# Trunk kernel: where twenty row sums, the column jobs and the first expert weights stand around the attention

## The chip, the cores and the metric

The kernel runs on one core of a Trainium2 chip, in one launch. The metric is the device time of that launch in microseconds (us); the times below are those of the core.

## What is computed

```python
for i in range(2):                       # DEPTH
    ml = silu(c) @ mod_w[i] + mod_b[i]   # (1024) @ (1024, 6144): shifts, scales and gates
    sh1, sc1, g1, sh2, sc2, g2 = split(ml, 6)
    hl = xl * (1 + sc1) + sh1
    yl = differential_attention(hl, context) if i == 0 else pooling(hl)
    xl = layer_norm(ALPHA * xl + (1 + g1) * yl)
    y2 = moe(xl * (1 + sc2) + sh2)       # 16 experts, top 2, three 1024 x 1024 matrices each
    xl = layer_norm(ALPHA * xl + (1 + g2) * y2)
```

There are 256 latent and 256 context tokens of width 1024, all in float32. The weights of 2 x 16 experts are most of what is read.

## The kernel before

All large weights come in **units** of 2 MB (128 x 4096 float32, 2.10 million bytes) into a buffer `ring` of 11 slots. An expert is 6 units, so layer 0 has the units 0 to 95 and unit v goes into slot `FREE[v % 11]`. SyncE (SP) issues all these loads in one fixed order, `LOADS` and then expert by expert, and waits ahead of each (`slot_free`, `early_used`) until its slot is free. One load that waits holds back all behind it.

The vector c @ mod_w is not multiplied on TensorE but summed on VectorE (DVE): a **sum** takes one unit of mod_w (two halves of 1 MB, slots 2 and 3 in turn) and adds its eight 128 x 512 blocks, each times a column of c (`unit_sum`, `half_sum`, L1340 and L1342). There are 20 of them, numbered 0 to 19. TensorE (PE) then folds four sums at a time over the partitions into bank 7 (`row_batch`, L638), `rows_sum` adds the bias (L1359), and small PE products and DVE copies bring the rows into the forms that are needed later: the **jobs** (`job`, `job_out`): columns (`cols_0`), a part of the router (`rpart_0`), the gates (`gt_0`, `g1_0`, `g1_1`). The early part of the kernel runs so:

- projections for k, q and v in groups of 7 us on PE, while DVE makes the first `EARLY_SUMS` sums and two rotary batches (`rope_batch`, L1380 to L1383);
- 16 attention **steps** s (`STEPS`): in each, PE makes a further projection group (steps 0 to 9 only), the scores of step s (L722), the transposes of s-2 (L582) and the values of s-3 (L740, bank 5). DVE takes maxima (L1469), forms the difference of the two softmaxes (L1480) and, in steps 0 to 9, one sum. ScalarE (ACT) takes exponentials (L1166), copies the transposes (L1160) and squares and copies the values (L1174, L1176);
- the heads are normed and turned, and multiplied with attn_wo in four products `project(t, h)` (L759); DVE makes sums 18 and 19 beside them;
- the first layer norm, the router (`route`), and then the experts (L902 gathers, L910 products).

The engines run their own lists in order, and semaphores join them. Loads can run ahead of the experts by the 11 slots at most, since unit v + 11 waits until unit v is used (`used`).

## Time and profile before

| | |
|---|---|
| device time, 3 runs | 1201.13 us (1200.76 to 1202.65) |
| the profiled execution's own time | 1202.47 us |
| its span in the trace | 1200.6 us |
| PE / DVE / ACT busy | 94% / 30% / 14% |
| read from HBM | 476.18 MB |
| granted PE clock, mean | 0.983 |

Busy shares are over the whole span. The times in the rows are counted from the span's start. The attention, the experts and the change of layer have different limits, so the mean shares say little.

### The profile page before, as it was taken

What the parts mean: (1) busy time and instruction counts of PE and PEld (TensorE: products, weight loads), DVE (VectorE), ACT (ScalarE), POOL (GpSimd) and SP (SyncE); (2) the same over time, 40 slices, a digit from 0 to 9 for tenths busy, and PEclk for the clock granted to TensorE, in tenths of its full rate; (3) what the DMA queues carried; (4) which work ended last, traced back from release to release, by engine and by line L of the source; (5) the groups of instructions that cost most, each with busy time, mean ns of one, the idle gap of its engine ahead of it and who ended that gap; (6) DMA issues with size and microseconds to landing.
All of it is one profiled execution on the core that took longest, in us unless ns stands there. A gap on an engine that the chain in (4) does not pass through costs nothing.

```text
span 1200.6 us, 12399 instructions
## 1 busy us (share of the span) xinstructions
PE 1133.3 (94%) x5282; PEld 493.3 (41%) x5282; DVE 362.8 (30%) x733; ACT 166.8 (14%) x397; POOL 8.0 (1%) x10
## 2 busy tenths in 40 slices
PE   8997998899999999999998889999999999988986
PEld 3543554545444333343333227543333433333322
DVE  1569899663111111111111115212111111111113
ACT  1201233514100000001000005200000100000000
POOL 0000000000000000000000010000000000000000
PEclk9998999899999999999999999999999999999999
DMA  9999897983999999999999999999999999999994
GB/s 387 407 376 379 289 361 269 400 321 158 431 429 430 433 429 430 430 431 430 431 430 430 431 424 430 424 429 432 431 429 432 430 430 433 430 430 430 431 430 182
DMA packets 41017, 480.17 MB, mean 400 GB/s; under 512 B 5120, under 2 KB 6400, under 8 KB 9472
## 3 DMA queue, kind: packets, MB, share of 16 engines
q1 hardware_dynamic: 39904, 476.91, 94.7%
q10 hardware_dynamic: 1056, 2.43, 0.7%
q8 instruction: 44, 0.72, 0.2%
q14 instruction: 13, 0.11, 0.0%
HBM read 476.18 MB, written 1.05 MB: 397 GB/s over the span
## 4 chain that ended last, share of the span: by engine, by line
PE 74%; DMA 18%; DVE 6%; ACT 1%; issue 1%; another core or an unknown queue 0%; SPq 0%; DVEq 0%
PE ps L910 44%; DMA ring<-in_moe_wu 16%; PE ps L902 5%; PE ps L918 4%; PE ps L664 3%; DMA ring<-in_mod_w 2%; PE ps L759 2%; PE ps L667 2%; DVE ring L1342 1%; PE ps L722 1%; PE ps L607 1%; PE ps L670 1%; PE ps L740 1%; DVE modp L1342 1%; PE ps L928 1%; PE ps L582 1%
## 5 line engine op out<-in xcount | busy, mean ns | idle before, releaser
L910 PE MATMUL ps<-ring,tra 128*64 128x512 f32 x2048 | 453.9, 597 | 24.2 <-DMA ring<-in_moe_wu 19.3
L910 PEld LDWEIGHTS ps<-ring,tra 128*64 128x64 f32 x2048 | 147.6, 138 | 322.3 <-issue 281.1
L910 PE MATMUL ps<-ring,work 128*64 128x512 f32 x1024 | 226.8, 595 | 1.9 <-DVE work L1693 1.9
L910 PEld LDWEIGHTS ps<-ring,work 128*64 128x64 f32 x1024 | 71.6, 137 | 135.6 <-issue 133.3
L1237 ACT ACTIVATE work<-ps 128x512 f32<-128x512 f32 x32 | 19.1, 597 | 506.5 <-PE ps L910 506.5
L1691 DVE TENSOR_TENSOR work<-work,ps 128x512 f32<-128x512 f32 x32 | 22.0, 687 | 205.7 <-PE ps L910 205.7
L1230 ACT ACTIVATE tra<-ps,cols 128x128 f32<-128x128 f32 x128 | 48.1, 456 | 255.3 <-PE ps L902 255.3
L1688 DVE TENSOR_TENSOR work<-ps,work 128x512 f32<-128x512 f32 x32 | 22.1, 691 | 202.1 <-ACT work L1237 202.1
L902 PEld LDWEIGHTS ps<-extra,xn 128*128 128x128 f32 x512 | 61.0, 195 | 24.3 <-issue 22.7
L902 PE MATMUL ps<-extra,xn 128*128 128x128 f32 x512 | 66.9, 285 | 1.4 <-DVE extra L1601 1.4
L918 PE MATMUL ps<-work,extra 64*128 64x512 f32 x256 | 63.6, 615 | 1.6 <-DVE work L1697 1.6
L664 PE MATMUL ps<-ring 128*128 128x512 f32 x128 | 58.6, 608 | 0.0
L1697 DVE TENSOR_TENSOR work<-ps,gt 128x512 f32<-128x512 f32 x16 | 11.1, 691 | 107.9 <-PE ps L910 107.9
L1697 DVE TENSOR_TENSOR work<-ps,rows 128x512 f32<-128x512 f32 x16 | 11.1, 691 | 107.9 <-PE ps L910 107.9
L1342 DVE SCALAR_TENSOR_TENSOR ring<-ring,cols 128x512 f32<-128x512 f32 x56 | 42.1, 752 | 2.1
L1693 DVE COPY work<-ps 128x512 f32<-128x512 f32 x32 | 22.1, 691 | 51.0 <-PE ps L928 51.0
L664 PEld LDWEIGHTS ps<-ring 128*128 128x128 f32 x128 | 24.0, 194 | 31.8 <-issue 31.8
L1342 DVE SCALAR_TENSOR_TENSOR extra<-ring,cols,extra 128x512 f32<-128x512 f32 x42 | 31.6, 752 | 3.9 <-DMA ring<-in_mod_w 2.5
L1342 DVE SCALAR_TENSOR_TENSOR modp<-ring,cols,modp 128x512 f32<-128x512 f32 x42 | 31.6, 752 | 1.5
L918 PEld LDWEIGHTS ps<-work,extra 64*128 64x128 f32 x256 | 22.0, 186 | 22.0 <-issue 15.1
L1676 DVE COPY extra<-ps 128x256 f32<-128x256 f32 x32 | 13.6, 424 | 48.4 <-PE ps L934 48.4
L667 PE MATMUL ps<-ring 128*128 128x512 f32 x64 | 28.1, 592 | 0.0
(192 smaller groups left out, 729.2 us busy)
## 6 DMA issues: line engine op xcount, KB each, us to landing
ring<-in_moe_wg SPq DMA_DIRECT2D x64, 2048.0 KB, 29.6
ring<-in_moe_wu SPq DMA_DIRECT2D x63, 2048.0 KB, 29.7
ring<-in_moe_wd SPq DMA_DIRECT2D x63, 2048.0 KB, 30.0
ring<-in_mod_w SPq DMA_DIRECT2D x40, 1024.0 KB, 9.6
ring<-in_mod_w SPq DMA_DIRECT2D x4, 2048.0 KB, 17.1
ring<-in_attn_wqkv SPq DMA_DIRECT2D x4, 2048.0 KB, 11.4
ring<-in_attn_wo SPq DMA_DIRECT2D x2, 2048.0 KB, 11.2
ring<-in_tokens SPq DMA_DIRECT2D x4, 512.0 KB, 18.0
```

What stands on the lines that cost most here:

```text
L664: return mm(bank(acc_bank(g)), w[:, k, t * P:t * P + P], hT[:, k, :], start=first, stop=end)
L667: return mm(bank(acc_bank(g)), hT[:, k, t * P:t * P + P], rhs, start=first, stop=end)
L759: last = mm(bank(2 * t + h), oT[t][:, k, :], wo[:, k, :], start=(k == 0), stop=(k == KT - 1))
L902: last = mm(bank(bk, 0, P, k * P, k * P + slots), xn[:, c0:c0 + P], sgat[:, t, 0:slots], start=(t == 0), stop=(t == TT - 1), skip_group_ch ...
L910: last = mm(ps[SLOTS * h:SLOTS * h + SLOTS, b, :], lhs(k0 + k), w[:, k, h * NB:(h + 1) * NB], start=(k0 + k == 0), stop=(k0 + k == KT - 1) ...
L918: last = mm(bank(2 * t + h), sw[SLOTS * h:SLOTS * h + SLOTS, t * P:t * P + P], ysb[SLOTS * h:SLOTS * h + SLOTS, :], start=False, stop=True ...
L1230: nc.scalar.activation(xg[i // 2 % 2][:, kk, :], bank(bk, k * P, k * P + P), ACT.Identity, bias=one(bcol[2 * layer], kk, 1), scale=one(aco ...
L1342: ins = v_.scalar_tensor_tensor(out=acc, in0=w[:, k, :], scalar=ck, in1=acc, op0=ALU.mult, op1=ALU.add)
L1688: v_.tensor_tensor(hmid, bank(4), sig, ALU.mult).then_inc(sem("silu_ready"), 1)
L1691: v_.tensor_tensor(hmid, hmid, bank(5), ALU.mult).then_inc(sem("h_ready"), 1)
L1693: v_.tensor_copy(work[:, NB:2 * NB], bank(7)).then_inc(sem("hTt_copied"), 1)
L1697: v_.tensor_tensor(ysb, bank(6), gt[layer], ALU.mult).then_inc(sem("ys_ready"), 1)
```

## The change

The tables that set the order get other numbers. Seven sums stand ahead of the steps and nine in the steps 0 to 8; both rotary batches come ahead of sum 5. Of the other four, sums 16 and 17 follow the norm of the heads, sum 18 is split between the attention's norm and the router, and sum 19 is made in the first expert, in slot 3 itself, and folded by a job of its own (`row_1`). The column jobs leave the steps and go between the projections; fold 4 goes behind the router's logits. Values alternate between banks 5 and 6, ACT copies before it squares, and DVE makes the last copy of transposes. Units 1 to 9 are now issued among the last sums. Unit 10, whose slot sum 19 holds, is issued behind unit 15.

```diff
-FREE = (10, 4, 8, 5, 9, 6, 7, 2, 3, 1, 0)
+FREE = (10, 4, 8, 5, 9, 6, 7, 1, 0, 2, 3)
...
-BATCH_AT = {6: 0, 10: 1, 15: 2, 19: 3}
-
-EARLY_SUMS = 8
-STEP_SUMS = 10
-
-LOADS = [("q", 0), 0, 1, ("v", 0), 2, "rows", 3, 4, ("k", 1), 5, 6, 7, 8, ("q", 1), 9, "ahead", 10, 11, 12, ("v", 1), 13, 14,
-         ("wo", 0), 15, 16, 17, ("wo", 1), "x", 18, 19]
-AHEAD = 1
-
-
-JOBS = ("cols_0", "rpart_0", "gt_0", "g1_0", "g1_1", "cols_2", "cols_1", "joint_0", "joint_1", "rpart_1", "gt_1",
+BATCH_AT = {8: 0, 12: 1, 16: 2, 20: 3}
+
+EARLY_SUMS = 7
+STEP_SUMS = 9
+ROPES_AT = 5
+
+LOADS = [("q", 0), 0, 1, ("v", 0), 2, "rows", 3, 4, ("k", 1), 5, 6, ("q", 1), 7, "ahead", 8, 9, 10, 11, ("v", 1), 12, 13,
+         ("wo", 0), 14, 15, "x", 16, 17, ("wo", 1), ("e", 1), ("e", 2), ("e", 3), ("e", 4), ("e", 5), ("e", 6), 18, 19,
+         ("e", 7), ("e", 8), ("e", 9)]
+AHEAD, ISSUED = 1, 10
+LATE_UNIT = 10
+AFTER_UNIT = 15
+
+
+JOBS = ("g1_0", "g1_1", "cols_0", "rpart_0", "gt_0", "row_1", "cols_2", "cols_1", "joint_0", "joint_1", "rpart_1", "gt_1",
         "lng_0", "lng_1", "lnb_0", "lnb_1")
-JOB_AT = {10: (0,), 11: (1,), 12: (2,)}
-JOB_BANK = (6, 6, 6, 2, 2, 7, 7, 7, 7, 7, 7, 7, 7, 7, 7)
-HEAD_BANK = ((6, 3), (4, 5))
+JOB_BANK = (2, 2, 6, 6, 5, 7, 7, 7, 7, 7, 7, 7, 7, 7, 7, 7)
+HEAD_BANK = ((1, 3), (4, 5))
 EARLY_JOBS = 5
-LATE_JOB = {(0, e): EARLY_JOBS + e - 1 for e in range(1, 7)} | {(1, e): EARLY_JOBS + 5 + e for e in range(1, 5)}
+LATE_JOB = {(0, e): EARLY_JOBS + e for e in range(7)} | {(1, e): EARLY_JOBS + 6 + e for e in range(1, 5)}
...
+        last_sum = ring[:, 3 * UNIT:3 * UNIT + NB]
...
                 elif v in (7, 8):
-                    sp.wait_ge(sem("half_summed"), 2 * (NSUM - 8 + v))
-                elif v < RING:
-                    sp.wait_ge(sem("unit_used"), NA - RING + v + 1)
+                    early_used(sp, ("wo", v - 7))
+                elif v == 9:
+                    sp.wait_ge(sem("half_summed"), 2 * (NSUM - 1))
+                elif v == LATE_UNIT:
+                    sp.wait_ge(sem("job_done"), EARLY_JOBS + 1)
...
-                for n in range(AHEAD if layer == e == 0 else 0, EU):
-                    load_unit(layer, e, n)
+                for n in range(EU):
+                    v = first_unit(layer, e) + n
+                    if v >= ISSUED and v != LATE_UNIT:
+                        load_unit(layer, e, n)
+                    if v == AFTER_UNIT:
+                        load_unit(0, LATE_UNIT // EU, LATE_UNIT % EU)
...
+                elif isinstance(what, tuple) and what[0] == "e":
+                    load_unit(0, what[1] // EU, what[1] % EU)
...
-                pe.wait_ge(sem("half_summed"), 2 * (BATCH * b + BATCH))
+                units = min(BATCH, NSUM - 1 - BATCH * b)
+                pe.wait_ge(sem("half_summed"), 2 * (BATCH * b + units))
                 if b == SUMS0 // BATCH:
                     pe.wait_ge(sem("rows_ready"), 1)
-                for g in range(4):
+                for g in range(units):
...
-                pe.wait_ge(sem("aT_copied"), s + 1)
+                if s < NS - 1:
+                    pe.wait_ge(sem("aT_copied"), s + 1)
+                else:
+                    pe.wait_ge(sem("last_aT_copied"), 1)
                 out_of_psum(9 if j == 0 else 19)
-                if s:
-                    pe.wait_ge(sem("o_copied"), s)
+                if s >= 2:
+                    pe.wait_ge(sem("o_squared"), s - 1)
                 for k in range(KEYT):
-                    last = mm(bank(5, 0, P, 0, P), aT[s % 2][:, k * P:k * P + P], vv[:, k, hh * P:hh * P + P],
+                    last = mm(bank(5 + s % 2, 0, P, 0, P), aT[s % 2][:, k * P:k * P + P], vv[:, k, hh * P:hh * P + P],
...
-                    pe.wait_ge(sem("job_out"), EARLY_JOBS)
-                pe.wait_ge(sem("oT_copied"), 2 * (t + 1))
+                    pe.wait_ge(sem("job_out"), 2)
                 for k in range(KT):
+                    if k % 4 == 0:
+                        pe.wait_ge(sem("oT_copied"), 2 * t + k // 4 + 1)
...
+                elif kind == "row":
+                    pe.wait_ge(sem("half_summed"), 2 * NSUM)
+                    r0 = C_ROW + 31 - SUMS[NSUM - 1][1] // 4
+                    last = mm(bank(bk, 96, 128), cst[:, r0:r0 + 32], last_sum, start=True, stop=True, skip_group_check=True)
...
                     values(NS - 3)
+                    pe.wait_ge(sem("exp_done"), 2 * NS)
+                    job(0)
                     turn_probs(NS - 1)
                     values(NS - 2)
                     turn_heads(0)
                     values(NS - 1)
-                    job(3)
                     project(0, 0)
                 elif s < NS:
                     if s >= 2:
                         turn_probs(s - 2)
                     if s >= 3:
                         values(s - 3)
-                for i in JOB_AT.get(s, ()):
-                    job(i)
-            pe.wait_ge(sem("aT_copied"), NS)
-            pe.wait_ge(sem("o_copied"), NS)
+            job(1)
+            pe.wait_ge(sem("o_squared"), NS)
+            job(2)
             turn_heads(1)
             project(0, 1)
-            job(4)
-            row_batch(4)
-            NT_BANK = (4, 6, 5, 7)
+            job(3)
+            NT_BANK = ((4, 6, 5, 0), (4, 6, 5, 7))
...
             project(1, 0)
-            turn_normed(0, 0)
+            job(4)
             project(1, 1)
-            pe.wait_ge(sem("rows_ready"), 2)
...
+                if layer == 0:
+                    pe.wait_ge(sem("job_out"), EARLY_JOBS)
+                turn_normed(layer, 0)
+                keep_clock(5 if layer else 1, 3)
                 turn_normed(layer, 1)
-                keep_clock(0, 1)
+                keep_clock(1, 1)
...
+                if layer == 0:
+                    row_batch(4)
...
+            def copy_probs(s):
+                act.wait_ge(sem("aT_done"), s + 1)
+                nc.scalar.copy(aT[s % 2], bank(4)).then_inc(sem("aT_copied"), 1)
+
+            def copy_values(s):
+                j, t, h = STEPS[s]
+                hh = HPJ * j + h
+                o = bank(5 + s % 2, 0, P)
+                act.wait_ge(sem("pv_done"), s + 1)
+                nc.scalar.copy(osb[:, t, hh * P:hh * P + P], o).then_inc(sem("o_copied"), 1)
+                act.wait_ge(sem("o_copied"), s + 1)
+                nc.scalar.activation(o, o, ACT.Square, accum_out=ss[:, t, hh:hh + 1]).then_inc(sem("o_squared"), 1)
+
+            for s in range(NS):
                 for kind, i in FILL[s]:
                     if kind == "g":
                         evacuate(i)
-                if 2 <= s < NS + 2:
-                    act.wait_ge(sem("aT_done"), s - 1)
-                    nc.scalar.copy(aT[s % 2], bank(4)).then_inc(sem("aT_copied"), 1)
-                if s < NS:
-                    act.wait_ge(sem("nb_ready"), s + 1)
-                    for n in range(2):
-                        j, t, h = STEPS[s]
-                        total = lead[:, t, HPJ * j + h:HPJ * j + h + 1] if n == 0 else sm[:, s % 2, 1:2]
-                        nc.scalar.activation(pr[s % 2][:, n, :], bank(score_bank(s) + n), ACT.Exp,
-                                             bias=nb[:, s % 2, n:n + 1], scale=SCALE, accum_out=total).then_inc(sem("exp_done"), 1)
-                if s == NS - 1:
-                    heads_std(0)
-                if s >= 3:
-                    j, t, h = STEPS[s - 3]
-                    hh = HPJ * j + h
-                    act.wait_ge(sem("pv_done"), s - 2)
-                    nc.scalar.activation(bank(5, P, 2 * P), bank(5, 0, P), ACT.Square,
-                                         accum_out=ss[:, t, hh:hh + 1]).then_inc(sem("o_squared"), 1)
-                    nc.scalar.copy(osb[:, t, hh * P:hh * P + P], bank(5, 0, P)).then_inc(sem("o_copied"), 1)
-                if s == NS + 1:
-                    copy_heads(0)
+                if s >= 2:
+                    copy_probs(s - 2)
+                act.wait_ge(sem("nb_ready"), s + 1)
+                for n in range(2):
+                    j, t, h = STEPS[s]
+                    total = lead[:, t, HPJ * j + h:HPJ * j + h + 1] if n == 0 else sm[:, s % 2, 1:2]
+                    nc.scalar.activation(pr[s % 2][:, n, :], bank(score_bank(s) + n), ACT.Exp,
+                                         bias=nb[:, s % 2, n:n + 1], scale=SCALE, accum_out=total).then_inc(sem("exp_done"), 1)
+                if 3 <= s < NS - 1:
+                    copy_values(s - 3)
+            heads_std(0)
+            copy_probs(NS - 2)
+            copy_values(NS - 4)
+            copy_values(NS - 3)
+            copy_heads(0)
+            copy_values(NS - 2)
+            copy_values(NS - 1)
...
-                if n == 6:
-                    rope_batch(0)
+                if n == ROPES_AT:
+                    for batch in range(2):
+                        rope_batch(batch)
                 unit_sum(n)
-            rope_batch(1)
...
-                for i in JOB_AT.get(s, ()):
-                    job_out(i)
                 if s == NS - 1:
                     heads_variance(0)
                 if s == NS:
                     norm_heads(0)
-            job_out(3)
+            dve.wait_ge(sem("aT_done"), NS)
+            v_.tensor_copy(aT[(NS - 1) % 2], bank(4)).then_inc(sem("last_aT_copied"), 1)
+            dve.wait_ge(sem("pv_done"), NS - 1)
+            job_out(0)
             heads_variance(1)
             norm_heads(1)
-            for n in range(EARLY_SUMS + STEP_SUMS, NSUM):
-                unit_sum(n)
-            job_out(4)
+            unit_sum(NSUM - 4)
+            job_out(1)
+            job_out(2)
+            unit_sum(NSUM - 3)
+            job_out(3)
...
+                        if (t, h) == (1, 0):
+                            half_sum(2 * (NSUM - 2))
                     spread(0, t)
                     deviation(0, t)
                     if t == 0:
-                        rows_sum(1)
+                        job_out(4)
...
+                if layer == 0:
+                    half_sum(2 * (NSUM - 2) + 1)
...
+                dve.wait_ge(sem("row_done"), -(-NSUM // BATCH))
                 pick_rows(0, 0)
                 pick_rows(1, 1).then_inc(sem("sgat_ready"), 1)
                 pick_weights(0).then_inc(sem("ssc_ready"), 1)
+                if layer == 0:
+                    rows_sum(1)
...
+                if layer == 0:
+                    rows_scaled()
...
+                if q == 0:
+                    half_sum(2 * (NSUM - 1))
...
+                if q == 0:
+                    half_sum(2 * (NSUM - 1) + 1)```

The DVE's list ahead of the steps (a sum is a row `TENSOR_SCALAR` and a row `SCALAR_TENSOR_TENSOR` x7, a rotary batch three rows `TENSOR_TENSOR`). Before, from sum 5:

```order
L1340 TENSOR_SCALAR ring<-ring,cols 128x512
L1342 SCALAR_TENSOR_TENSOR ring<-ring,cols 128x512 x7
L1380 TENSOR_TENSOR ring<-ring 128x4x256
L1382 TENSOR_TENSOR ring<-ring 128x1024
L1383 TENSOR_TENSOR ring<-ring 128x4x256
L1340 TENSOR_SCALAR ring<-ring,cols 128x512
L1342 SCALAR_TENSOR_TENSOR ring<-ring,cols 128x512 x7
L1340 TENSOR_SCALAR ring<-ring,cols 128x512
L1342 SCALAR_TENSOR_TENSOR ring<-ring,cols 128x512 x7
L1380 TENSOR_TENSOR ring<-ring 128x1024
```

These are sum 5, batch 0, sums 6 and 7, and the start of batch 1. And now, from sum 4, which both have:

```order
L1371 TENSOR_SCALAR ring<-ring,cols 128x512
L1373 SCALAR_TENSOR_TENSOR ring<-ring,cols 128x512 x7
L1412 TENSOR_TENSOR ring<-ring 128x4x256
L1414 TENSOR_TENSOR ring<-ring 128x1024
L1415 TENSOR_TENSOR ring<-ring 128x4x256
L1412 TENSOR_TENSOR ring<-ring 128x1024
L1414 TENSOR_TENSOR ring<-ring 128x1024
L1415 TENSOR_TENSOR ring<-ring 128x1024
L1371 TENSOR_SCALAR ring<-ring,cols 128x512
```

Both batches, which the scores of step 0 wait for, stand ahead of sum 5, and there is one sum less.

SP's loads from attn_wo's first half on (`in_mod_w` halves are sums, `in_moe_*` are expert units). Before:

```order
L429 DMA ring<-in_attn_wo 128x4096
L429 DMA ring<-in_mod_w 128x2048 x6
L429 DMA ring<-in_attn_wo 128x4096
L429 DMA xn<-in_x 128x2x1024
L429 DMA ring<-in_mod_w 128x2048 x4
L429 DMA ring<-in_moe_wg 128x4096
L429 DMA ring<-in_moe_wu 128x4096 x2
L429 DMA ring<-in_moe_wd 128x4096 x2
```

And now:

```order
L433 DMA ring<-in_attn_wo 128x4096
L433 DMA ring<-in_moe_wg 128x4096
L433 DMA ring<-in_moe_wu 128x4096 x2
L433 DMA ring<-in_moe_wd 128x4096 x2
L433 DMA ring<-in_moe_wg 128x4096
L433 DMA ring<-in_mod_w 128x2048 x4
L433 DMA ring<-in_moe_wg 128x4096
L433 DMA ring<-in_moe_wu 128x4096 x2
L433 DMA ring<-in_moe_wd 128x4096
L433 DMA ring<-in_moe_wg 128x4096 x2
L433 DMA ring<-in_moe_wu 128x4096 x2
L433 DMA ring<-in_moe_wd 128x4096 x3
```

Units 1 to 6 went ahead of the sums 18 and 19, and the last row holds the units 10, 16 and 17.

PE's list from the turned heads on (L759 and L774 are the projections, 8 matmuls each; L638 and L651 folds). Before:

```order
L582 MATMUL ps<-cst,ring 128x128 x8
L759 MATMUL ps<-ring,work 128x512 x8
L781 MATMUL ps<-rows,cst 128x512
L638 MATMUL ps<-modp,cst 32x512 x2
L638 MATMUL ps<-extra,cst 32x512 x2
L759 MATMUL ps<-ring,tra 128x512 x8
L582 MATMUL ps<-cst,xn 128x128 x8
L759 MATMUL ps<-ring,tra 128x512 x8
L607 MATMUL ps<-cst 128x512 x3
```

And now:

```order
L774 MATMUL ps<-ring,work 128x512 x8
L796 MATMUL ps<-rows,cst 128x512
L781 MATMUL ps<-cst,rows 128x28 x4
L594 MATMUL ps<-cst,ring 128x128 x8
L774 MATMUL ps<-ring,work 128x512 x8
L824 MATMUL ps<-cols,rwa 32x1 x8
L774 MATMUL ps<-ring,tra 128x512 x8
L815 MATMUL ps<-rows,cst 64x512 x2
L774 MATMUL ps<-ring,tra 128x512 x8
L594 MATMUL ps<-cst,xn 128x128 x8
L619 MATMUL ps<-cst 128x512 x3
```

The fold and the turn of the normed rows (L582 from xn) left the space between the projections, and three column jobs (L781, L824, L815) came in.

## Rows read from the trace of the kernel before

**Rows 1.** Windows: busy of PE, PEld, DVE, ACT, POOL; PE clock, DMA share, GB/s.

```profile
274.00:292.00 18.00, 16.67 (x119) 11.77 (x120) 8.01 (x41) 9.54 (x22) 0.00 (x0) 0.93 0.01 2
292.00:593.00 301.00, 300.06 (x1499) 121.41 (x1495) 50.44 (x118) 25.22 (x60) 0.00 (x0) 1.00 1.01 429
...
716.00:760.00 44.00, 40.59 (x250) 32.28 (x252) 21.62 (x71) 20.98 (x39) 2.00 (x2) 0.96 1.01 430
```

**Rows 2.** Timeline of SP: start, time over the merged issues.

```profile
267.13 24.35 SPq L429 DMA_DIRECT2D ring<-in_moe_wd  x2
```

**Rows 3.** Chain that ended last: start, time, what.

```profile
597.03 44.54 DMA ring<-in_moe_wu
...
1120.81 49.09 DMA ring<-in_moe_wu
```

**Rows 4.** Timeline of DVE ahead of the steps; [idle before].

```profile
77.10 5.56 DVE L1342 SCALAR_TENSOR_TENSOR ring<-ring,cols 128x512 f32<-128x512 f32 x7
86.73 0.49 DVE L1340 TENSOR_SCALAR ring<-ring,cols 128x512 f32<-128x512 f32 x1 [4.07 <-DMA ring<-in_mod_w]
...
92.65 1.22 DVE L1380 TENSOR_TENSOR ring<-ring 128x1024 f32<-128x1024 f32 x1
...
96.18 0.48 DVE L1340 TENSOR_SCALAR ring<-ring,cols 128x512 f32<-128x512 f32 x1
```

**Rows 5.** Timeline of PE up to step 1.

```profile
75.06 0.62 PE L638 MATMUL ps<-modp,cst 128*32 128x512 f32 x2 [1.72 <-DVE extra L1342]
...
108.14 1.07 PE L638 MATMUL ps<-ring,cst 128*32 128x512 f32 x8 [4.34 <-DVE ring L1342]
111.67 2.08 PE L722 MATMUL ps<-ring 64*128 64x512 f32 x4 [2.46 <-DVE ring L1383]
113.67 8.29 PE L664 MATMUL ps<-ring 128*128 128x512 f32 x16
121.89 1.13 PE L722 MATMUL ps<-ring 64*128 64x512 f32 x4
```

**Rows 6.** Timeline of DVE: the maxima of steps 1, 9, 10, 13, 15.

```profile
123.06 1.22 DVE L1469 TENSOR_REDUCE small<-ps 128x2 f32<-128x1024 f32 x1 [1.86 <-PE ps L722]
...
198.23 1.22 DVE L1469 TENSOR_REDUCE small<-ps 128x2 f32<-128x1024 f32 x1 [0.17 <-PE ps L722]
...
206.58 1.22 DVE L1469 TENSOR_REDUCE small<-ps 128x2 f32<-128x1024 f32 x1
...
218.33 1.22 DVE L1469 TENSOR_REDUCE small<-ps 128x2 f32<-128x1024 f32 x1 [0.37 <-PE ps L722]
...
224.05 1.22 DVE L1469 TENSOR_REDUCE small<-ps 128x2 f32<-128x1024 f32 x1 [0.65 <-PE ps L722]
```

**Rows 7.** Window of the steps 10 to 15, columns as in rows 1.

```profile
200.00:224.00 24.00, 20.62 (x113) 12.46 (x110) 20.39 (x43) 13.56 (x47) 0.00 (x0) 0.79 1.01 426
```

**Rows 8.** Timeline of ACT behind the last step.

```profile
226.98 1.28 ACT L1144 ACT_TABLE_LOAD   x1
...
228.81 0.59 ACT L1160 COPY tra<-ps 128x512 f32<-128x512 f32 x1
```

**Rows 9.** Timeline of PE from the last steps to the fourth projection.

```profile
202.68 1.94 PE L766 MATMUL ps<-cst,rows 128*128 128x28 f32 x8
...
235.60 7.03 PE L759 MATMUL ps<-ring,work 128*128 128x512 f32 x16
...
250.21 1.02 PE L781 MATMUL ps<-rows,cst 128*128 128x512 f32 x2
...
260.07 7.03 PE L759 MATMUL ps<-ring,tra 128*128 128x512 f32 x16
```

**Rows 10.** Timeline of DVE at the router.

```profile
277.35 0.19 DVE L1619 TENSOR_TENSOR small<-ps,rb 128x32 f32<-128x32 f32 x1 [3.78 <-PE ps L876]
```

**Rows 11.** Timeline of PE from the ranks to the first expert.

```profile
281.48 0.84 PE L886 MATMUL ps<-small,cst 128*128 128x16 f32 x6
...
287.47 13.95 PE L910 MATMUL ps<-ring,tra 128*64 128x512 f32 x64
```

More of the change, by code:

```diff
@@ L1152, in copy_heads @@
                                          ACT.Copy, scale=subln).then_inc(sem("oT_copied"), 1)
-            for s in range(NS + 3):
+            def copy_probs(s):
[10 more added lines that the diff above has]
+            for s in range(NS):
                 for kind, i in FILL[s]:
@@ L1417, in job_out @@
                     v_.tensor_copy(gt[int(w)], src).then_inc(sem("job_out"), 1)
+                elif kind == "row":
+                    part = rows[1][96:128, :]
+                    dve.wait_ge(sem("rows_ready"), 2)
+                    v_.tensor_tensor(part, part, ps[96:128, JOB_BANK[i], :], ALU.add).then_inc(sem("job_out"), 1)
                 elif kind == "lnb":
@@ L1525, in normed_out @@
                 dve.wait_ge(sem("nT_done"), 4 * layer + 2 * t + 2)
-                v_.tensor_copy(nT[:, 4:8, t * P:t * P + P], bank((6, 7)[t]).rearrange("p (k t) -> p k t", k=4))\
+                v_.tensor_copy(nT[:, 4:8, t * P:t * P + P], bank((6, 0 if layer == 0 else 7)[t]).rearrange("p (k t) -> p k t", k=4))\
                     .then_inc(sem("nT_dve"), 1)
@@ L1671, in route @@
                 weights_out(NE * layer)
+                if layer == 0:
+                    rows_scaled()
             def weights_out(q):
```

26 lines of the change are left out of this document (11 added, 15 removed).

## Prediction, on record before the run

> **What bounds the kernel now.** I read the windows first. From 292 us on the DMA engines run at share 1.01 and 429 GB/s, also while the layers change, whatever PE does [rows 1]. The chain that ended last confirms it: from 597 us it waits for expert weights, and again from 1121 us to the last units [rows 3]. PE starts with a full ring, uses experts faster than they come, has eaten up its stock by 597 us, and from there each unit's arrival sets the pace. So the end is fixed by one thing: the time at which the stream of loads last stood still, and how much was loaded by then. All loads behind that point follow without a gap.
>
> The stream last stands still from 274 to 292 us: share 0.01 [rows 1]. SP's row says why. It issues unit 10 at 267.1 and its next, unit 11, 24.3 us later [rows 2], because unit 11 needs the slot of unit 0. All 11 slots are full, and the first expert must use one. Its first products start at 287.47 [rows 11]. So idle DMA in the attention costs nothing by itself. **What counts is T, the start of the first expert, and the number of units ahead of it.** If T moves by x and n units fewer are loaded by then, the end moves by x plus n times 2.10 MB / 429 GB/s = 4.9 us.
>
> **What the change does to T**, from front to back. The shift is against the times before; minus is earlier.
>
> *A, start of the steps.* Before, PE ended its group of step 0 at 108.14 - 4.34 = 103.8, then waited 4.34 us for sum 7 (the fold of sums 4 to 7) and 2.46 us for batch 1; it had also waited 1.72 us for the fold of sums 0 to 3 [rows 5]. Now the first fold stands two groups later, the second in step 2, and both batches ahead of sum 5: sum 4 ends at 77.10 + 5.56 = 82.7, two batches of 3.5 us (92.65 to 96.18) end at 89.7 [rows 4], long before the scores. These start at 103.8 - 1.7 = 102.1 in place of 111.67. DVE is ready as well: two sums of 5.9 us (86.73 to 92.65) behind 89.7 end at 101.6 [rows 4]. The 4.07 us wait for sum 5's load is filled by the batches. Then the clock. The scores after the wait took 2.08 us against 1.13 in step 1, and the next group 8.29 against 7.03 for 16 matmuls of the same shape [rows 5, 9]. Without the wait step 1's scores end at 102.1 + 1.1 + 7.0 + 1.1 = 111.3 in place of 123.0. Shift -11.7.
>
> The Trainium skill (TensorE: Matmul & The Clock Gate, the section What's actually happening) says the same of the cause: an idle array falls to half clock, 1.2 of 2.4 GHz, and work brings it back. By it there is no ramp left at 103 us. The trace agrees so far as the rows behind the wait are the slow ones.
>
> *B, steps 1 to 10.* From step 1's maxima to step 9's there are 75.2 us [rows 6]; content is the same (8 sums, 2 batches, 2 folds), so -11.7 holds at step 9. Step 9 loses its sum: before, step 10's maxima came 8.35 us later. DVE would need 8.35 - 5.9 = 2.45, but PE must make scores, a transpose, values and now fold 3: three times about 1.0 and 0.5. I take 3.5, so -4.9. Shift -16.6.
>
> *C, steps 10 to 15.* 17.5 us for five steps, with three column jobs and a PE clock of 0.79 [rows 6, 7]. The two steps without a job, 218.33 to 224.05, took 2.86 us each. Five of them are 14.3; ACT's exponentials and copies now have one semaphore more in each step, so I take 15.0. Bounds: 14.3, and 17.5 if nothing is won. -2.5. Shift -19.1.
>
> *D, last maxima to first projection.* 11.55 us before (224.05 to 235.60) [rows 6, 9]. Job `g1_0` (1.0 us) moves in front of the last transpose, into the time in which PE waits for the table load of 1.28 us at 226.98 and the copy at 228.81 [rows 8]; the last copy goes to DVE; the values of two steps no longer share a bank; and the projection starts on half of the turned heads. Following ACT from the exponentials: table 1.3, root 0.2, copy 0.6, then transpose 0.9, values 1.0, heads 0.9, values 1.0 on PE: 8.8. -2.8, bounds 0 and -3.5. Shift -21.9: the first projection starts at 213.7.
>
> The copy at 228.81 starts 0.55 us after the table load is over [rows 8]. The Trainium skill (ScalarE: Activation LUTs, What ACT_TABLE_LOAD costs) adds a drain of about 1.4 us to each switch of tables; by that D would be -1.4 and the time 1.4 us longer. No such gap stands in the rows, so I leave it out.
>
> *E, the four projections.* From 235.60 to 260.07 + 7.03 = 267.1 [rows 9]. Out: the fold between them (1.0) and the turn of the normed rows (1.0, now in the wait behind the fourth projection). `g1_1` (1.02) stays. In: `cols_0` (1.0; at most the 1.94 of its row), `rpart_0` 0.4 and `gt_0` 1.0. +0.5, at most +1.4. Is DVE late anywhere? By my estimate from the same row lengths the heads are normed about 4 us behind the start of the first projection, sum 16 and `cols_0` end at 225.5, sum 17 at 231.5, and the t = 0 half of the norm at 236.5, all before PE needs them. Then `gt_0` out at 239, 2.2 us of gating, and the half sum of sum 18, 3.0: to 244.3. The fourth projection ends at 245.7. The cover is about 1.4 us thin; beyond it each us delays T. Shift -21.4.
>
> *F, norm, router, first expert.* The second half of sum 18 (3.0) lies in DVE's 3.78 us wait for the logits [rows 10]. Fold 4 (three matmuls, 0.75) stands ahead of PE's 16 residual products, whose end met the ranks at 281.48 [rows 11] without a gap: +0.8. `rows_sum` (0.75) lies beside the gather. Shift -20.6: **T = 266.9**.
>
> *G, units ahead.* Unit 10 is no longer loaded ahead of T: slot 3 holds sum 19. The 11 slots hold 10 units, so the stream has 2.10 MB less behind it when it goes on: **+4.9 us**. Is the stream still full by then? The last three slots come free at the end of the third and fourth projection (238.2, 245.7) and with sum 18 (277.35 - 0.7 - 21 = 256), and 4.9 us each end at 261, nine before T + 3.5 = 270.4. So DMA will idle again.
>
> Behind T: unit 15 is issued when unit 4 is used (T + 21), unit 10 when `row_1` is done (T + 25.5), and DMA has units 11 to 15 until T + 29. Unit 10 lands by T + 36, and the second expert needs it at T + 43. Sum 19's two halves lie in DVE's waits for products there.
>
> **Sum.** -11.7 - 4.9 - 2.5 - 2.8 + 0.5 + 0.8 + 4.9 = -15.7 us. Against the profiled execution's own 1202.47 (span 1200.6 and 1.9 around it) this gives 1186.8; it stood 1.3 above the median of the runs, so for the median 1201.13 - 15.7 = 1185.4. What no row covers (semaphores between the thinner waits) makes things rather later: I say 1186.
>
> **Rivals.**
> - *The attention gives less back.* In steps 1 to 9 PE and DVE both are full, and C, D and the thin cover in E rest on waits that get shorter. With C and D at zero and 1.5 us of DVE in E: -15.7 + 2.5 + 2.8 + 1.5 = -8.9, time 1192. For it: no row shows steps without these waits. Against: the two undisturbed steps at 2.86. 0.15.
> - *The slot costs nothing.* If the stream were not full at T before the change, or is not after it, G is no loss; time 1180.5. Against: 18 us of idle at share 0.01. 0.05.
> - *More is won.* C at 14.3, D at -3.5, E at 0, no delay in F: 1182 to 1183.5. 0.10.
> - *Slower.* Sum 18 is now issued behind units 3 to 6, on an SP queue that goes in order, and unit 6 waits for the turned heads (223.5). DVE has its first half inside the layer norm, in front of everything to T. It should land at 232 and is wanted at 241. Each us beyond 241 + 1.4 delays T; it decides from 15.7 us beyond, a landing at 258. For it: four waits ahead in one queue. Against: nothing in the queue is asked for later than 224. Similarly unit 10 behind `row_1` would have to stop the stream for 16 us. 0.03; near no change 0.02.
>
> **How the numbers follow.** The forecast as summed has 0.65. The range for 8 in 10 takes in the gain of the third rival and the loss of the first: 1181.5 to 1193. A measurement of this kernel can tell about 0.2% (2.4 us) from no change. Faster by more than that: 0.65 + 0.15 + 0.05 + 0.10 = 0.95; within it 0.02; slower 0.03.
>
> **What would show it.** A: no wait over 1 us before the first scores, which start near 102, and full clock there. B and C: last maxima near 205. D and E: first projection near 214, fourth over near 246. F: first expert products near 267. G: DMA share about 0 from 262 to 271, then 1.01 with no gap at T + 25, and SP waiting for the first expert with 10 units issued. The first expert 20.6 us earlier and the end only 15.7 earlier is the mark of the lost slot. Wrong would be: a DMA gap in the first two experts, DVE waiting for a `mod_w` load in the norm, or the end moving with something other than T.

## The result and the profile after

The changed kernel takes 1183.8 us (median of 4 runs, 1183.2 to 1185.0), the kernel before 1201.4 in the same session. The ratio is 0.9853, interval [0.9836, 0.9870]: 1.5% faster. The forecast said 1186.0 with a range of 1181.5 to 1193.0. The profiled execution has a span of 1181.8 us and its own time is 1183.56; before these were 1200.6 and 1202.47. So they fell by 18.8 and 18.9, where the prediction's sum said 15.7.

The windows, at the places that answer to [rows 1, 7], columns as there:

```profile
182.00:206.00 24.00, 22.72 (x136) 13.68 (x135) 22.19 (x46) 17.94 (x55) 0.00 (x0) 1.00 0.92 371
...
255.00:262.00 7.00, 6.28 (x57) 6.18 (x56) 5.17 (x28) 2.55 (x5) 0.00 (x0) 1.00 0.63 264
262.00:268.00 6.00, 6.00 (x37) 3.02 (x37) 2.17 (x8) 2.68 (x8) 0.00 (x0) 1.00 0.00 0
268.00:274.00 6.00, 6.00 (x32) 2.00 (x30) 2.57 (x4) 0.60 (x1) 0.00 (x0) 1.00 0.98 369
274.00:574.00 300.00, 297.51 (x1484) 119.19 (x1482) 54.78 (x125) 24.65 (x59) 0.00 (x0) 1.00 1.01 430
700.00:742.00 42.00, 38.95 (x247) 31.53 (x247) 22.49 (x73) 22.09 (x42) 0.00 (x0) 0.96 1.01 429
```

The window of the steps 10 to 15 now has a granted PE clock of 1.00 in place of 0.79 [rows 7]. The stream of loads last stands still from 262 to 268 (share 0.00) and then runs at 1.01 and 430 GB/s, also while the layers change. SP shows the same pause: unit 9 is the second issue of the first row, unit 11 comes when the first expert gives back a slot, and unit 10 is one of the three of the last row.

```profile
243.54 9.76 SPq L433 DMA_DIRECT2D ring<-in_moe_wu  x2
267.26 0.33 SPq L433 DMA_DIRECT2D ring<-in_moe_wd  x1
...
289.24 3.92 SPq L433 DMA_DIRECT2D ring<-in_moe_wd  x3
```

DVE's maxima of the steps 1, 9, 10 and 15, which answer to [rows 6]:

```profile
110.73 1.22 DVE L1505 TENSOR_REDUCE small<-ps 128x2 f32<-128x1024 f32 x1 [0.62 <-PE ps L735]
...
186.64 1.22 DVE L1505 TENSOR_REDUCE small<-ps 128x2 f32<-128x1024 f32 x1
189.43 1.23 DVE L1505 TENSOR_REDUCE small<-ps 128x2 f32<-128x1024 f32 x1 [0.27 <-PE ps L735]
...
202.46 1.23 DVE L1505 TENSOR_REDUCE small<-ps 128x2 f32<-128x1024 f32 x1
```

PE, which answers to [rows 5, 9, 11]: the scores of step 0, the first projection, `cols_0`, the fourth projection, fold 4 and the first expert.

```profile
101.43 1.13 PE L735 MATMUL ps<-ring 64*128 64x512 f32 x4
...
210.81 7.03 PE L774 MATMUL ps<-ring,work 128*128 128x512 f32 x16
218.54 1.82 PE L781 MATMUL ps<-cst,rows 128*128 128x28 f32 x8
...
236.38 7.13 PE L774 MATMUL ps<-ring,tra 128*128 128x512 f32 x16
...
253.01 0.62 PE L651 MATMUL ps<-modp,cst 128*32 128x512 f32 x2 [0.70 <-DVE extra L1373]
...
263.56 13.95 PE L930 MATMUL ps<-ring,tra 128*64 128x512 f32 x64
```

T, the start of the first expert, is 263.56 in place of 287.47: 23.9 us earlier. The end is 18.8 us earlier. The difference of 5.1 is the lost slot. In the chain that ended last, the waits for weights have moved forward; the last answers to that at 1120.81 in [rows 3]:

```profile
576.23 46.27 DMA ring<-in_moe_wu
...
1101.66 49.43 DMA ring<-in_moe_wu
```

### The profile page after: what moved, and what is told of

The parts are those of the page before. It is cut to its first block, busy times and chain, and to the rows that moved or that the text cites. A ratio compares the mean times of both kernels' runs of the same rounds, so it can differ in the third digit from the quotient of the medians.

```text
span 1181.8 us, 12403 instructions
## 1 busy us (share of the span) xinstructions
PE 1124.6 (95%) x5282; PEld 487.8 (41%) x5282; DVE 364.2 (31%) x735; ACT 167.0 (14%) x396; POOL 8.0 (1%) x10
## 4 chain that ended last, share of the span: by engine, by line
PE 75%; DMA 20%; DVE 3%; ACT 0%; issue 0%; another core or an unknown queue 0%; SPq 0%; DVEq 0%
PE ps L930 42%; DMA ring<-in_moe_wu 20%; PE ps L677 5%; PE ps L680 5%; PE ps L922 5%; PE ps L938 4%; PE ps L774 2%; PE ps L683 2%; PE ps L735 1%; PE ps L948 1%; PE ps L594 1%; PE ps L756 1%; PE ps L872 1%; PE ps L954 1%; DMA ring<-in_mod_w 1%; PE ps L627 1%
## 5 line engine op out<-in xcount | busy, mean ns | idle before, releaser
L930 PE MATMUL ps<-ring,tra 128*64 128x512 f32 x2048 | 454.5, 598 | 27.6 <-DMA ring<-in_moe_wu 22.0
L930 PEld LDWEIGHTS ps<-ring,tra 128*64 128x64 f32 x2048 | 146.5, 138 | 327.7 <-issue 281.9
L930 PE MATMUL ps<-ring,work 128*64 128x512 f32 x1024 | 226.8, 595 | 1.9 <-DVE work L1743 1.9
L930 PEld LDWEIGHTS ps<-ring,work 128*64 128x64 f32 x1024 | 71.6, 137 | 135.6 <-issue 133.3
L1373 DVE SCALAR_TENSOR_TENSOR ring<-ring,cols 128x512 f32<-128x512 f32 x63 | 47.4, 752 | 2.2
L1373 DVE SCALAR_TENSOR_TENSOR modp<-ring,cols,modp 128x512 f32<-128x512 f32 x42 | 31.6, 752 | 1.5
L683 PE MATMUL ps<-ring 128*128 128x256 f32 x128 | 28.1, 379 | 0.0
```

Source lines behind the costliest of these rows:

```text
L683: last = mm(bank(acc_bank(g), 0, P, n * TOK, (n + 1) * TOK), w[:, k, hd * P:hd * P + P], hT[:, k, 0:TOK], start=first and n == 0, stop=end ...
L930: last = mm(ps[SLOTS * h:SLOTS * h + SLOTS, b, :], lhs(k0 + k), w[:, k, h * NB:(h + 1) * NB], start=(k0 + k == 0), stop=(k0 + k == KT - 1) ...
L1373: ins = v_.scalar_tensor_tensor(out=acc, in0=w[:, k, :], scalar=ck, in1=acc, op0=ALU.mult, op1=ALU.add)
```

## The experiments

Each edits the changed kernel and computes the same. Ratios are against the kernel before, run in the same session (sessions 1 to 3: 1203.88, 1202.49 and 1202.28 us). "Base" is the changed kernel: span 1181.8, T 263.56. In the diffs "..." stands for lines left out.

Spans and T are read from one traced execution of each kernel. The medians, less base's 1183.8, give e1 +4.7, e2 +5.6, e3 +7.0, e4 +8.5, e5 +8.3, e6 +2.6, e7 +3.8, e8 +8.4 and e10 +14.5. The traced executions of e6, e7 and e8 are the lowest of theirs, so their span shifts are at the low end. The kernel before varied by 2.5 us between sessions (1201.4 to 1203.9), so ratios of different sessions can't be compared more finely than 0.2%.

### Is the end T plus 4.9 us for each unit not loaded ahead?

**One unit fewer ahead**, e1_nine_ahead: unit 9 waits for the slot of unit 0.

```diff
-         ("e", 7), ("e", 8), ("e", 9)]
-AHEAD, ISSUED = 1, 10
+         ("e", 7), ("e", 8),]
+AHEAD, ISSUED = 1, 9
...
                 elif v == 9:
                     sp.wait_ge(sem("half_summed"), 2 * (NSUM - 1))
+                    used(sp, 0)
```

> Unit 9 is no longer issued among the last sums but waits, like unit 11, until the first expert has used unit 0. Nothing in front of the experts changes. By my account (end = T less 4.9 us for each unit loaded ahead) the first expert's products stay at 263.6 us, the stream of loads has 2.10 MB more behind its last standstill, and the time is 1183.8 + 4.9 = 1188.7 us. The rival, that PE's own stock of loaded units matters little because the end is set by when PE starts, gives 1183.8.

1188.5 us, ratio 0.9877 [0.9862, 0.9892]. T is 263.63, as in base, and the span 1186.8: +5.0 for one unit. SP now waits from 243.6 to 267.7:

```profile
243.61 24.10 SPq L433 DMA_DIRECT2D ring<-in_moe_wu  x2
```

Term G holds, to 0.1 us.

**A later first expert**, e2_late_expert: five filler products in front of it, nothing else.

```diff
+                if layer == 0:
+                    pe.wait_ge(sem("routed"), 1)
+                    keep_clock(5, 5)
                 for e in range(NE):
                     expert(layer, e)
```

> Five more matmuls of 128x512 (0.91 us each as the fillers at 244.22 show) stand in front of the first expert of layer 0; their result is not used. T moves by 4.5 us, 10 units stay ahead. My account gives 1183.8 + 4.5 = 1188.3 us. Rival: PE waits for weights some 40 us in all later on, so it has room and 4.5 us of extra PE work ahead of the experts are swallowed: 1183.8.

1189.4 us, 0.9878 [0.9863, 0.9893]; T 269.48 (+5.9) and span 1187.7 (+5.9). The end moves with T, one for one. Here are PE's router products (3.84 us in base), the fillers and the first expert:

```profile
253.99 5.46 PE L872 MATMUL ps<-cst,work 128*128 128x128 f32 x32
265.09 4.46 PE L619 MATMUL ps<-cst 128*128 128x512 f32 x10
269.48 5.80 PE L930 MATMUL ps<-ring,tra 128*64 128x512 f32 x26
```

4.5 of the 5.9 us are the fillers. The rest was lost ahead of them, where the same 32 products took 1.6 us longer: the granted clock is 0.73 from 255 to 260, and 1.00 there in base.

**The ring not full at T**, e3_units_behind: the units 1 to 6 are issued behind the sums 18 and 19, as the kernel before had its sums first.

```diff
-         ("wo", 0), 14, 15, "x", 16, 17, ("wo", 1), ("e", 1), ("e", 2), ("e", 3), ("e", 4), ("e", 5), ("e", 6), 18, 19,
+         ("wo", 0), 14, 15, "x", 16, 17, ("wo", 1), 18, 19, ("e", 1), ("e", 2), ("e", 3), ("e", 4), ("e", 5), ("e", 6),
```

> Units 1 to 6 are issued behind sums 18 and 19, as before the change; all else stays. T stays at 263.6 us. By my account the ring must also be full at T + 3.5: sum 19's second half can be issued at 228.1, then nine units of 4.9 us end at about 274.5, where the stream of the changed kernel restarts at about 269: 5.5 us later, 1189.3 us, and no standstill ahead of the experts. If T alone decides: 1183.8. If the late sums delay DVE in the norm it would be the other way, T a little earlier, as sum 18 lands earlier.

1190.8 us, 0.9908 [0.9885, 0.9931]; T 263.58, unchanged, but span 1188.9 (+7.1; I had expected +5.5). The four half loads of the sums hold up the queue for 11.4 us while free slots stand empty behind them, and after that the windows have no pause (from 228 to 268 the DMA share is 1.01, and the last three are shown). Of its four runs one took 1196.1 us, the others 1190.5 to 1190.8. Why it is 1.6 us more than I had expected stays open.

```profile
217.09 11.38 SPq L433 DMA_DIRECT2D ring<-in_mod_w  x4
```

```profile
255.00:260.00 5.00, 4.28 (x39) 4.18 (x38) 3.68 (x22) 2.23 (x4) 0.00 (x0) 1.00 1.03 436
260.00:265.00 5.00, 5.00 (x41) 4.02 (x41) 3.66 (x16) 2.82 (x8) 0.00 (x0) 1.00 0.99 426
265.00:270.00 5.00, 5.00 (x26) 1.63 (x24) 0.00 (x0) 0.19 (x1) 0.00 (x0) 1.00 0.99 423
```

So the rule has a condition, that the ring is full before T, and this change meets it by its order of issue.

### What the parts of the change are worth

**One bank for the values**, e4_one_bank: the jobs stay where the change put them.

```diff
-                if s >= 2:
-                    pe.wait_ge(sem("o_squared"), s - 1)
+                if s:
+                    pe.wait_ge(sem("o_squared"), s)
...
-                    last = mm(bank(5 + s % 2, 0, P, 0, P), aT[s % 2][:, k * P:k * P + P], vv[:, k, hh * P:hh * P + P],
+                    last = mm(bank(5, 0, P, 0, P), aT[s % 2][:, k * P:k * P + P], vv[:, k, hh * P:hh * P + P],
...
-                o = bank(5 + s % 2, 0, P)
+                o = bank(5, 0, P)
```

> Values use bank 5 only again, and TensorE waits until ScalarE has squared the step before; all else as changed. If the alternating banks are what made the steps 10 to 15 take 13.0 us instead of my 15.0, they go back to 14.5 to 15 and the two values in front of the first projection wait for ScalarE as well (+1.5): the first expert at 263.6 + 3.3, time about 1187. If the banks matter only at the end: +1.5, 1185.3. If the pace came from the jobs and the clock: no change in the steps.

A miss in the time: 1192.3 us, 0.9913 [0.9896, 0.9929]; span 1190.6, +8.8. Steps 10 to 15 take 14.74 us against 13.03 (+1.7), as expected, at a granted clock of 1.00. From the last maxima (204.11) to the first projection (218.12) it is 14.0 against 8.35 (+5.7, where I had said +1.5). Another 1.6 us are lost at the router, as in e2 (5.47 us in place of 3.84). PE's timeline says why the last stretch grows: behind the last step it waits twice for ACT's square of the values before it may write the next ones into the only bank.

```profile
209.73 1.33 PE L756 MATMUL ps<-ring,tra 128*128 128x128 f32 x8 [2.37 <-ACT ps L1187]
210.85 1.92 PE L796 MATMUL ps<-rows,cst 128*128 128x512 f32 x2
...
217.16 1.13 PE L756 MATMUL ps<-ring,tra 128*128 128x128 f32 x8 [1.57 <-ACT ps L1187]
218.12 4.46 PE L774 MATMUL ps<-ring,work 128*128 128x512 f32 x10
```

In base the same values show no wait at all, and the job at L796 takes 1.02. The waits make idle PE, and the job behind the first runs at 1.92. I had costed the wait alone. Of the 5.7 the two waits are 3.9; the rest I can't split further. The kernel before, with one bank too, took 11.55 us for this stretch [rows 6, 9], less than the 14.0 here. So 5.7 is what the second bank is worth in the changed order, not its share of what the change gained.

**One bank, and the jobs back in steps 10 to 12**, e5_jobs_in_steps, on top of the last edit:

```diff
+JOB_AT = {10: (0,), 11: (1,), 12: (2,)}
-JOBS = ("g1_0", "g1_1", "cols_0", "rpart_0", "gt_0", "row_1", "cols_2", "cols_1", "joint_0", "joint_1", "rpart_1", "gt_1",
+JOBS = ("cols_0", "rpart_0", "gt_0", "g1_0", "g1_1", "row_1", "cols_2", "cols_1", "joint_0", "joint_1", "rpart_1", "gt_1",
...
-JOB_BANK = (2, 2, 6, 6, 5, 7, 7, 7, 7, 7, 7, 7, 7, 7, 7, 7)
+JOB_BANK = (6, 6, 6, 2, 2, 7, 7, 7, 7, 7, 7, 7, 7, 7, 7, 7)
...
```

> As the one-bank kernel, and the three column jobs are back in steps 10, 11, 12 (out of the space between the projections). The step without a sum stays. Before the change the three steps with jobs took 11.75 us against 2.6 each now: +3.9 us in the steps, and 1.7 + 0.3 + 1.0 = 3.0 us come back between the projections, so +0.9 against the one-bank kernel if those 11.75 us were the jobs' own. If most of them were the half clock that followed TensorE's wait for sum 17 in step 9, which is gone here, the steps grow by 1.5 us at most and the kernel is 1.5 us faster than the one-bank one.

1192.1 us, 0.9915 [0.9899, 0.9932]; span 1189.8, 0.8 less than with one bank alone. The steps get 3.1 us longer (189.21 to 207.06) and the way to the first projection 1.3 (to 222.34). The projections, without the jobs, get 3.3 shorter, and PE's 32 router products at L872 take 3.84 us, where with one bank alone they took 5.47. Without that last difference, which the edit doesn't touch, this kernel would be 0.9 us slower than the one-bank one, what the first theory said. The second theory is out: the steps grow by 3.1 us and not by 1.5 at most, at a granted clock of 1.00. So moving the jobs is worth 0.9 us at most by itself (the medians differ by 0.2). It frees the second bank, and the two together are worth 8 us. With the jobs in the steps, but no sum in step 9, the clock stays at 1.00, so the jobs alone don't bring the 0.79 of [rows 7].

```profile
190.00:207.00 17.00, 15.97 (x105) 10.30 (x106) 13.28 (x34) 12.12 (x39) 0.00 (x0) 1.00 0.91 389
205.00:222.00 17.00, 11.91 (x63) 9.29 (x63) 7.82 (x18) 9.07 (x27) 0.00 (x0) 0.80 0.63 255
```

**A sum back into step 9**, e8_sum_in_step9:

```diff
-STEP_SUMS = 9
+STEP_SUMS = 10
...
-            unit_sum(NSUM - 4)
```

> The changed kernel with a tenth sum put back into step 9 of the attention, as the kernel before had it, and taken out of those behind the steps. Theory: from step 9 to step 10 the maxima now go 2.8 us apart, and with a sum of four 1.46 us operations in front of them they go 8.3 to 9 us apart; TensorE waits inside that step, and its clock may fall in the steps behind it for another 1 to 2 us; the sums behind the steps stand beside other work, so nothing comes back there: the first expert starts 6 to 7 us later and the time is about 1190.5 us. Rival: the sum only changes its place, and what VectorE loses in step 9 it has less to do behind the steps: 1183.8 us.

1192.2 us, 0.9919 [0.9904, 0.9934]; span 1189.2 (+7.4), T 270.92 (+7.4, a little over the 6 to 7 that I had expected). The maxima of step 9, the sum (its seven operations) and the maxima of step 10, and the windows around them:

```profile
186.62 1.22 DVE L1505 TENSOR_REDUCE small<-ps 128x2 f32<-128x1024 f32 x1
189.58 5.48 DVE L1373 SCALAR_TENSOR_TENSOR modp<-ring,cols,modp 128x512 f32<-128x512 f32 x7
194.97 1.22 DVE L1505 TENSOR_REDUCE small<-ps 128x2 f32<-128x1024 f32 x1
```

```profile
190.00:198.00 8.00, 2.34 (x14) 1.39 (x13) 7.68 (x13) 2.13 (x7) 0.00 (x0) 0.79 1.03 441
198.00:206.00 8.00, 7.90 (x44) 5.61 (x42) 5.63 (x13) 5.89 (x20) 0.00 (x0) 0.78 0.93 393
```

The step takes 8.35 us again instead of 2.8 (+5.6). PE stands idle for 5.7 us of the first window, whose mean clock is 0.79, and though it is busy for 7.9 of the next 8 us, it is so at a mean of 0.78: the half clock, 1.2 of 2.4 GHz, up to 201 and the full one from 202 on. Steps 10 to 15 take 14.88 (+1.8). The rival, that the sum only changes its place, is out.

Is this wait also the source of the 0.79 of [rows 7]? That isn't shown. In the kernel before, PE has jobs to do beside sum 17. From 200.82 to 206.47 no row of it waits more than 0.24 us, and the clock is at half from 205 on, before its wait of 2.70 us begins at 206.47. Here are the windows of the kernel before, columns as in [rows 1]:

```profile
200.00:205.00 5.00, 4.66 (x26) 3.59 (x24) 4.82 (x7) 2.09 (x8) 0.00 (x0) 0.98 0.97 407
205.00:210.00 5.00, 2.30 (x8) 0.71 (x4) 4.72 (x14) 1.88 (x7) 0.00 (x0) 0.50 1.01 427
210.00:215.00 5.00, 5.00 (x33) 3.22 (x32) 3.39 (x9) 2.46 (x8) 0.00 (x0) 0.50 1.04 439
215.00:220.00 5.00, 5.00 (x33) 3.18 (x33) 4.21 (x10) 3.26 (x10) 0.00 (x0) 1.00 1.02 431
220.00:225.00 5.00, 4.66 (x30) 2.75 (x27) 4.20 (x8) 4.45 (x16) 0.00 (x0) 1.00 0.96 410
```

The jobs without the sum leave the clock at 1.00 (e5), and the sum without the jobs halves it behind a wait of 5.66 us (e8). Why it fell in the kernel before, with both, stays open. Nor can its price there be read from the total: steps 10 to 15 took 17.5 us with it, and 17.85 in e5 without it.

**Eight sums ahead**, e7_eight_ahead (`EARLY_SUMS = 8`, `STEP_SUMS = 8`):

> Eight sums ahead of the steps and eight in steps 0 to 7, the folds where the changed kernel has them. VectorE reaches step 0 5.9 us later; the scores stand ready at 101.4. If VectorE's total work sets T, the 5.9 us are won back in step 8, which has no sum; TensorE, which has a group of 7 us ahead of each scores, hides most of the lateness: T +2, time 1185.8. If a sum ahead of the steps costs its full length (as term A counted it): T +5.9, 1189.7.

1187.6 us, 0.9895 [0.9865, 0.9925]; span 1184.8 (+3.0), T 266.68. The maxima of step 1 come 6.8 us later (117.55) and those of step 10 only 3.1 later (192.54): the step that loses its sum gives part of it back. In step 1 DVE also waits 1.80 us for the next sum's load (at 111.64), since the loads keep their order. A sum ahead of the steps costs half of its 5.9 us in this trace. The six runs reach from 1186.7 to 1198.1, and their median lies midway between the two theories.

**The second rotary batch behind sum 6**, e6_ropes_last:

```diff
-                    for batch in range(2):
-                        rope_batch(batch)
+                    rope_batch(0)
                 unit_sum(n)
+            rope_batch(1)
```

> Batch 1 of the rotary work goes behind sum 6 again (batch 0 stays ahead of sum 5). VectorE has the same work and ends it at 102.3 us. TensorE is ready for the first scores at 101.4 and now has to wait for batch 1 until about 102.5: T +1.1 to +1.3 us, time 1185.0. If the place of the batches was what made the start of the steps early (the 10 us of term A), it would be +3.5 or more: 1187.5.

1186.4 us, 0.9875 [0.9859, 0.9892]; span 1183.1 (+1.3). The scores of step 0 wait 1.44 us for the batch, and T moves by 1.35, as expected. The median is less clear: the four runs reach from 1185.0 to 1189.2, the traced one took 1185.0, and the median of 1186.4 lies between the theory and its rival.

**A late load of sum 18**, e10_sums_behind_unit8. This makes the condition of the prediction's slower rival true.

```diff
-         ("wo", 0), 14, 15, "x", 16, 17, ("wo", 1), ("e", 1), ("e", 2), ("e", 3), ("e", 4), ("e", 5), ("e", 6), 18, 19,
-         ("e", 7), ("e", 8), ("e", 9)]
+         ("wo", 0), 14, 15, "x", 16, 17, ("wo", 1), ("e", 1), ("e", 2), ("e", 3), ("e", 4), ("e", 5), ("e", 6), ("e", 7), ("e", 8),
+         18, 19, ("e", 9)]
```

> The changed kernel with the loads of the sums 18 and 19 issued behind the units 7 and 8 and no longer ahead of them. It tests the slower rival of the prediction, a late load of sum 18 whose wait lies inside the norm. Theory: sum 18 is issued at about 244 us instead of 222, lands at 251 to 254, and VectorE, which takes its instructions in order, has the rows and the norm queued behind it: the first expert starts about 10 us later (1194.3 us), still less than before, since the ring is full by then. Rival: the sum's wait is covered by TensorE's projections: 1183.8 us.

1198.3 us, 0.9963 [0.9950, 0.9977]; span 1196.1 (+14.3), T 277.82 (+14.3; I had expected +10). DVE waits inside the norm, with everything to T queued behind:

```profile
254.13 0.49 DVE L1371 TENSOR_SCALAR extra<-ring,cols 128x512 f32<-128x512 f32 x1 [14.98 <-DMA ring<-in_mod_w]
```

In base this row starts at 239.27, 14.9 us earlier, and DVE then still waits 1.50 us for the fourth projection. That is the prediction's cover of 1.4. Beyond it each us counts: 13.4 us in the norm. The last 0.9 are at PE: after its wait of 14.6 us the turn of the normed rows took 1.97 us against 1.09 in base, the fillers behind it 1.56 against 1.02, and about 0.5 us came back in a shorter wait for DVE (0.24 against 0.70). The landing came at the late end of the 251 to 254 that I had said, and the 10 us went with the early end and without the clock. By these numbers the point at which the change would have given nothing is, as an estimate, a landing near 259 (254.1 and the 4.5 us between spans 1196.1 and 1200.6); the prediction said 258.

### A version that is faster than both

**Unit 10 ahead as well**, e9_unit10_ahead. The halves of sum 18 go into DVE's two waits in the norm, the first of sum 19 to the router, its second behind `rows_sum` and into another tile; then slot 3 is free ahead of T.

```diff
-         ("e", 7), ("e", 8), ("e", 9)]
-AHEAD, ISSUED = 1, 10
+         ("e", 7), ("e", 8), ("e", 9), ("e", 10)]
+AHEAD, ISSUED = 1, 11
...
-                    sp.wait_ge(sem("job_done"), EARLY_JOBS + 1)
+                    sp.wait_ge(sem("half_summed"), 2 * NSUM)
...
+                        to = sums[0] if n == NSUM - 1 and k >= 4 else acc
...
-                            half_sum(2 * (NSUM - 2))
+                            half_sum(2 * (NSUM - 2) + 1)
...
+                        half_sum(2 * (NSUM - 2))
...
-                    half_sum(2 * (NSUM - 2) + 1)
+                    half_sum(2 * (NSUM - 1))
...
+                    half_sum(2 * (NSUM - 1) + 1)
...
```

> Sum 19 leaves the first expert: sum 18's halves move into DVE's two waits in the norm (3.4 us for the gate job, 1.5 us for the fourth projection), sum 19's first half takes the place behind the normed rows, its second half stands behind the rows' sum at about 260 us and writes a tile outside slot 3, so unit 10 is issued at about 263.3 us in place of 289. T moves by about +1.4 us. By my account the stream stands still until 263.3 instead of 267.3 and has one unit less to come behind that: 1183.8 - 4.0 = 1179.8 us. If only T counts: 1185.2. If unit 10 ahead counts in full and T too: 1183.8 - 4.9 + 1.4 = 1180.3.

1180.2 us, 0.9805 [0.9792, 0.9819]; span 1178.9 (-2.9), T 264.01. To make sure that this isn't a difference between sessions, both kernels ran again side by side.

> The changed kernel itself, once more, on the chip and in the session of the next run, so that the two can be compared directly. Both theories: 1183.8 us, 0.985 of before.

> The version with unit 10 loaded ahead, once more, beside the changed kernel. Theory: one more unit ahead of the first expert is worth 4.9 us, less what the load loses while it is the only one in the queue (about 1.2 us) and what the waits in the norm cost (about 0.5 us): 1180.2 to 1180.9 us, 2.9 us below the changed kernel. Rival: the difference of the first comparison was one of sessions, and the two are within 1 us.

The changed kernel: 1183.4 us, 0.9842 [0.9829, 0.9855], span 1181.5. With unit 10 ahead: 1180.7, 0.9821 [0.9808, 0.9834], span 1178.9. The gain stands at 2.7 us, and the five runs of each don't overlap. It is less than 4.9 for two reasons. Unit 10 is issued at 262.8, only 4.4 us ahead of the 267.3 at which base's stream goes on. And the queue then holds few loads: from 264 to 274 e9 moves 365 GB/s on average, not 430. Base restarts slowly too (262 GB/s from 268 to 270), but moves 434 GB/s from 270 to 272. By 278 e9 has moved 1.4 MB more than base, by my estimate worth 3.3 us at 429 GB/s. The first windows of e9:

```profile
264.00:266.00 2.00, 1.99 (x10) 0.90 (x12) 1.68 (x7) 0.26 (x1) 0.00 (x0) 1.00 0.81 303
266.00:268.00 2.00, 2.00 (x12) 0.79 (x10) 0.00 (x0) 0.00 (x0) 0.00 (x0) 1.00 0.96 410
```

## Why the prediction was right, step by step

The account (T, and the units loaded ahead of it) was right and was tested from three sides: T alone (e2), a unit alone (e1, e9) and the full ring (e3). In e4 to e8 and e10 too the end moved with T, within 0.2 us. The time came 2.2 us under the forecast. T moved by 23.9 us where the prediction had 20.6: A to D and F gave 4.7 us more than said, E and a stretch that I had at zero took 1.4 back. So part of the closeness is luck, since errors cancelled, and in C a cause was missing from the sum. Shifts are against the kernel before.

- **A**, start of the steps: forecast -11.7, measured -12.3 at step 1 (123.06 to 110.73). The scores start at 101.43 (forecast 102.1), in 1.13 us and thus at full clock, and none of PE's three waits of [rows 5] is left. Only the eighth sum and the batch were undone by themselves (e7, e6), the later folds not.
- **B**, steps 1 to 10: I had step 1 to step 9 unchanged. It took 75.9 us in place of 75.2, since a fold (PE, 1.07 us at 117.68) now stands in step 2, where PE has no slack: step 1 to step 2 is 9.1 us in place of 8.4. Step 9: forecast -4.9, measured -5.6 (8.35 to 2.8; I took 3.5). e8 gives it back.
- **C**, steps 10 to 15: 15.0 taken, 13.03 measured. This is the largest miss, 2.0 us, and 1.7 of it are the second bank. I built C on the two steps of 2.86 us without a job [rows 6]. They ran at full clock (1.00 from 215 to 225, in the windows under e8), but with one bank: PE waits 0.24 us at 221.82 for ACT to copy the values. In e4, with one bank, no jobs and a clock of 1.00, the five steps take 14.74, close to the 14.3 of these rows; base, with the second bank, takes 1.7 less. The prediction named the second bank only in D. The jobs' move is worth 3.1 us here (e5 against e4), so bank and jobs cover all of the 4.4 that C gained. The 1.8 of e8 are what a wait in step 9 would cost behind it, not a part of this miss.
- **D**, last maxima to first projection: 8.8 taken, 8.35 measured. Without the second bank the new order would be worse than the old one here, 14.0 us (e4) against 11.55. ACT goes on 0.02 us after its table load (below), so the drain of about 1.4 us that the Trainium skill adds (ScalarE: Activation LUTs, What ACT_TABLE_LOAD costs) isn't in this trace either.

```profile
205.39 1.28 ACT L1166 ACT_TABLE_LOAD   x1
206.69 0.21 ACT L1166 ACTIVATE small<-small 128x8 f32<-128x8 f32 x1
```

- **E**, projections: forecast +0.5, measured +1.2 (32.7 us from the start of the first to the end of the fourth). `cols_0` takes 1.82, not 1.0; its row before, 1.94, was the better guide. DVE's cover is 1.50 us (forecast 1.4), and e10 shows what lies beyond.
- **F**, norm to first expert: forecast +0.8, measured -0.3 (20.05 against 20.37). Fold 4 waits 0.70 us for DVE's half sum, but PE's clock is 1.00 where it was 0.93 [rows 1]. I costed the instructions and not the clock.
- **G**, a unit fewer ahead: forecast +4.9, measured +5.1 in the pair and +5.0 by e1.

Of the rivals, the slot is not free (e1). The slower one needs a landing near 259 (e10). In the changed kernel the first half load of sum 18 is issued at 221.67, and the four half loads take 10.1 to 12.0 us to land, so it is there by 233.7. The first, that the attention gives less back, fell at C and D. What came is nearest to the third, more is won.

What the parts give, each undone by itself: sum out of step 9 7.4, banks with the jobs' move 8.0, eighth sum 3.0, batch 1.3, together 19.7; less 5.0 for the slot 14.7 of the 18.8. By the medians the same parts are 8.4, 8.3, 3.8 and 2.6, less 4.7: 18.4 of 17.6. So the sum is good to some 4 us only, and the parts need not add up: each is what it is worth beside the others. The later folds (4.34 and 1.72 us of PE's waits in [rows 5]) and the last sum's move behind T were not undone by themselves.
